# The first half of the first norm: the row's gain on VectorE, its root in a diagonal on TensorE, with other banks and another order for the convolutions

## The chip, the cores and the metric

The kernel runs on one core of one Trainium2 chip. The metric is the device time of one execution in microseconds (us), and lower is better. A core has five engines that run their own instruction streams and wait for each other by semaphores: TensorE (PE in the profile, with its weight loads as PEld), VectorE (DVE), ScalarE (ACT), GpSimd (POOL) and SyncE (SP), which here issues the loads of the weights.

## The reference

A block of a language model and a second block behind it, for 256 tokens of 1024 features, all in fp32. What lies at the change is the start of the first block:

```python
h = rmsnorm(x, norm_mix[l])            # x * rsqrt(mean(x*x) + EPS) * gain, by row
(fq, fk, fv, ff, gq, gk, gv, gb, ga, gz, sq, sk, sv, gates) = split_projection(h @ w_in[l])
...
qkv = jax.nn.silu(causal_dwconv(jnp.concatenate([gq, gk, gv], axis=-1), gdn_conv[l]))   # 4 taps
cq, ck, cv = jnp.split(qkv, [GDN_KW, 2 * GDN_KW], axis=-1)
beta = jax.nn.sigmoid(gb.astype(f32))
g_log = -jnp.exp(gdn_a_log[l].astype(f32)) * jax.nn.softplus((ga + gdn_dt_bias[l]).astype(f32))
```

Behind it come three attentions, a cross attention and three feed-forward networks, which the change doesn't touch.

## The kernel before

**Products.** An fp32 product is made of three fast ones. Each weight is split into HI, its rounding to the fast type, and LO = RAW - HI, and so is the activation (XH, XL); XH·HI, XL·HI and XH·LO are added up in PSUM. The weights come in 187 blocks of 128 x 2048, numbered through all phases: blocks 0 to 5 are `gdn` (query, key and value of the convolution), 6 to 9 `sbqk`, 10 and 11 `sbv`. A block is loaded by SyncE in two halves into one of two RAW slots, ScalarE makes its HI and VectorE its LO in one of four ring places; `split_ahead(phase, Turn(j))` does this for the block four later. GpSimd makes LO of blocks 0, 5 and 7. SyncE issues the load of a half as soon as LO of the same half two blocks earlier is made, since that frees the RAW slot.

**Order.** There is no scheduler. Every engine's order is the order of the code in its own function, and semaphores join them. A bank of ACCP (four PSUM banks of 512 columns) takes the sums of one `gdn` or `sbqk` block; TensorE waits until the bank's last reader has finished. The small results go through the four banks of SMP in the fixed order of the list `SMALL`; each waits for the bank's user four places earlier. `gTk1` so waits for `tiny`, and `gTv0` for `gTq0`.

**The opening.** X is loaded in two tiles of 128 rows (t = 0, 1). For each, ScalarE sums the squares of the first 512 columns (b = 0) and VectorE those of the last 512 (b = 1). GpSimd adds the two and takes the power -1/2: the root of each row. TensorE meanwhile spreads the gain vector over all 128 rows by a product with a row of ones (two products, one for each 512 columns, counted by `gain_spread`), and makes some idle products, `spin`. `mix_scale(t, b)` on VectorE makes XS = X x root x gain, `mix_turn(t, b)` on TensorE transposes its four 128x128 tiles, `mix_split(t, b)` takes XH from them on ScalarE and then XL on VectorE. The order of the four parts is (0,0), (1,0), (0,1), (1,1). `first_gemm` starts when XH of both b = 0 parts and the first 512 columns of HI of block 0 (`first_hi`) are there.

**The convolution banks.** For each of the six `gdn` blocks j, ScalarE copies the sums to CONVF scaled by the last tap ("base"), two copies; VectorE adds the three other taps of both feature tiles from the bank, six linked steps at L2301, and frees the bank; ScalarE applies the silu. Between the steps stand the splits of block j + 4. The `tinyT` product behind block 4 makes the narrow columns, ScalarE copies them to TINY, TensorE turns them as `tiny`, and VectorE sums them up behind its splits. When all six silus are done, TensorE turns CONVF: `gTq0`, `gTq1`, `gTk0`, `gTk1` behind `sbqk` 0, `gTv0` and `gTv1` behind `sbqk` 1.

## Time and profile before

| | |
|---|---|
| median of 3 timed runs | 1151.31 us (1149.84, 1151.31, 3620.2) |
| profiled execution, own time | 1150.2 us |
| its span | 1148.5 us |
| TensorE busy | 1137.1 us, 99% of the span |
| VectorE, ScalarE, GpSimd busy | 741.6, 589.4, 105.7 us |
| granted clock of TensorE, mean | 0.999 |
| HBM traffic | 207.67 MB read, 182 GB/s over the span |

The span runs from the first to the last instruction of the profiled execution; 1.7 us lie around it. A busy time counts overlapping instructions once. One of the three timed runs is an outlier, so the median is the higher of the two others. The rows below give start and duration in us from the start of the span.

### The profile page before, as it was taken

How to read it: one execution, taken by the hardware profiler on the slowest of the kernel's cores; microseconds unless marked ns; L12 is line 12 of the kernel's file. 1: busy time of each engine (PE TensorE's matmuls, PEld its weight loads, DVE VectorE, ACT ScalarE, POOL GpSimd, SP SyncE). 2: the span in 40 equal slices, each digit the busy share in tenths (PEclk: the TensorE clock that was granted, in tenths of full speed). 3: DMA queues.
4: the chain of work that ended last, by engine and by line, in shares of the span. 5: the costliest groups of instructions: out<-in, count | busy, mean ns of one | idle time of the engine just before them, and what ended most of it. 6: DMA issues, size and time to landing. Idle time of an engine off the chain costs nothing.

```text
span 1148.5 us, 16462 instructions
## 1 busy us (share of the span) xinstructions
PE 1137.1 (99%) x6408; PEld 993.3 (86%) x6408; DVE 741.6 (65%) x931; ACT 589.4 (51%) x788; POOL 105.7 (9%) x162
## 2 busy tenths in 40 slices
PE   9999999999999999999999999999999999999997
PEld 8998888888889999988888898899888888889885
DVE  6866686657777888754664554665866566545465
ACT  5674654446565766543554443564554364444353
POOL 6410211000011000000000000200500010000020
PEclk9999999999999999999999999999999999999999
DMA  9643753455634765564665656465457467555641
GB/s 252 206 156 97 223 185 110 164 201 184 217 132 138 251 207 176 187 215 147 209 214 182 186 174 209 154 213 181 145 187 239 146 229 234 192 168 175 213 137 72
DMA packets 122894, 209.81 MB, mean 183 GB/s; under 512 B 10965, under 2 KB 58186, under 8 KB 122827
## 3 DMA queue, kind: packets, MB, share of 16 engines
q1 hardware_dynamic: 119225, 198.64, 54.2%
q10 hardware_dynamic: 3506, 10.23, 2.4%
q8 instruction: 47, 0.77, 0.3%
q0 software_dynamic: 96, 0.01, 0.1%
q14 instruction: 20, 0.16, 0.0%
HBM read 207.67 MB, written 1.18 MB: 182 GB/s over the span
## 4 chain that ended last, share of the span: by engine, by line
PE 94%; DVE 3%; DMA 1%; ACT 1%; issue 0%; POOL 0%; POOLq 0%; DVEq 0%; SPq 0%; ACTq 0%
PE ACCP L867 28%; PE ACCP L869 28%; PE ACCP L868 28%; PE SMP L1068 3%; DVE CONVF L2301 1%; PE SMP L1061 1%; DVE LO L2176 1%; DMA RAW<-in_w_in_dram 1%; DMA X<-in_x_dram 0%; PE SMP L1221 0%; PE SMP L1237 0%; PE SMP L1021 0%; PE SMP L1016 0%; PE SMP L1015 0%; PE SMP L1406 0%
## 5 line engine op out<-in xcount | busy, mean ns | idle before, releaser
L2176 DVE TENSOR_TENSOR LO<-RAW,HI 128x1024 fp32r<-128x1024 f32 x365 | 438.1, 1237 | 231.3 <-ACT HI L1607 225.0
L1607 ACT ACTIVATE HI<-RAW 128x1024 fp32r<-128x1024 f32 x366 | 370.1, 1054 | 269.6 <-PE ACCP L869 222.6
L867 PE MATMUL ACCP<-HI,XH 128*128 128x512 f32 x704 | 277.4, 394 | 0.0
L869 PE MATMUL ACCP<-HI,XL 128*128 128x512 f32 x704 | 274.4, 390 | 0.0
L868 PE MATMUL ACCP<-LO,XH 128*128 128x512 f32 x704 | 274.0, 389 | 0.0
L867 PE MATMUL ACCP<-XH,HI 128*128 128x256 f32 x640 | 182.0, 284 | 0.7 <-DVE CONVF L2301 0.7
L869 PE MATMUL ACCP<-XH,LO 128*128 128x256 f32 x640 | 181.1, 283 | 0.0
L868 PE MATMUL ACCP<-XL,HI 128*128 128x256 f32 x640 | 181.1, 283 | 0.0
L869 PEld LDWEIGHTS ACCP<-HI,XL 128*128 128x128 f32 x704 | 132.1, 188 | 27.8
L868 PEld LDWEIGHTS ACCP<-LO,XH 128*128 128x128 f32 x704 | 132.3, 188 | 26.2
L867 PEld LDWEIGHTS ACCP<-HI,XH 128*128 128x128 f32 x704 | 132.3, 188 | 26.2
L867 PE MATMUL ACCP<-HI,HH 128*128 128x512 f32 x328 | 128.1, 390 | 0.0
L868 PE MATMUL ACCP<-LO,HH 128*128 128x512 f32 x328 | 127.7, 389 | 0.0
L869 PE MATMUL ACCP<-HI,HL 128*128 128x512 f32 x328 | 127.6, 389 | 0.0
L867 PEld LDWEIGHTS ACCP<-XH,HI 128*128 128x128 f32 x640 | 122.8, 192 | 1.0 <-issue 0.8
L868 PEld LDWEIGHTS ACCP<-XL,HI 128*128 128x128 f32 x640 | 122.8, 192 | 0.1
L869 PEld LDWEIGHTS ACCP<-XH,LO 128*128 128x128 f32 x640 | 122.8, 192 | 0.0
L715 POOL TENSOR_SCALAR STAT<-STAT 128x1 f32<-128x1 f32 (+3 forms) x24 | 10.2, 426 | 755.1 <-ACT XS L1877 449.9
L869 PEld LDWEIGHTS ACCP<-HI,HL 128*128 128x128 f32 x328 | 61.6, 188 | 12.8
L867 PEld LDWEIGHTS ACCP<-HI,HH 128*128 128x128 f32 x328 | 61.6, 188 | 12.5
L868 PEld LDWEIGHTS ACCP<-LO,HH 128*128 128x128 f32 x328 | 61.6, 188 | 12.5
L1615 ACT ACTIVATE XH<-SMP 128x512 fp32r<-128x512 f32 x36 | 20.4, 596 | 35.4 <-PE SMP L1068 35.1
(416 smaller groups left out, 1144.5 us busy)
## 6 DMA issues: line engine op xcount, KB each, us to landing
RAW<-in_w_in_dram SPq DMA_DIRECT2D x104, 512.0 KB, 4.5
RAW<-in_w_up_dram SPq DMA_DIRECT2D x44, 512.0 KB, 4.4
RAW<-in_ffn_w_gate_dram SPq DMA_DIRECT2D x44, 512.0 KB, 4.6
RAW<-in_ffn_w_up_dram SPq DMA_DIRECT2D x44, 512.0 KB, 4.5
RAW<-in_ffn_w_down_dram SPq DMA_DIRECT2D x44, 512.0 KB, 4.4
RAW<-in_w_down_dram SPq DMA_DIRECT2D x22, 512.0 KB, 4.2
RAW<-in_w_out_dram SPq DMA_DIRECT2D x8, 512.0 KB, 4.4
RAW<-in_w_mkv_dram SPq DMA_DIRECT2D x8, 512.0 KB, 4.3
```

What stands on the lines that cost most here:

```text
L715: link(pool.tensor_scalar(mean_square, mean_square, EPS, None, ALU.add))
L867: pe.matmul(dst, lhs[0], rhs[0], start=start, stop=False)
L868: pe.matmul(dst, lhs[0], rhs[1], start=False, stop=False)
L869: return pe.matmul(dst, lhs[1], rhs[0], start=False, stop=stop)
L1061: last = pe.matmul(small(name)[:, h * P:(h + 1) * P], lhs, rhs, start=True, stop=True)
L1068: last = pe.transpose(small(name)[:, h * P:(h + 1) * P], source(h), IDENT[:, :])
L1607: act.activation(HI[:, n % RING, half_of(half)], RAW[:, n % RAWS, half, :], ACT.Copy).then_inc(hi_ready, 1)
L1615: act.activation(dst, src, ACT.Copy, scale=scale).then_inc(signal, 1)
L2176: dve.tensor_tensor(LO[:, s, c], RAW[:, n % RAWS, half, :], HI[:, s, c].bitcast(f32), ALU.subtract).then_inc(lo_ready[s], 1)
L2301: ins = dve.scalar_tensor_tensor(out=y, in0=u[:, 0:SEQ - back], scalar=col("gdn_conv", (3 - back) * 12 + tile), in1=y, op0=ALU.mult, op1=A ...
```

## The change

For b = 0 VectorE multiplies X by the gain alone (`mix_scale`), right behind the square of the same tile, with a wait for the first spreading product and for ScalarE's square (which uses XS as scratch). GpSimd multiplies the identity by the row's root behind each root, into a new tile ROOT_DIAG (a 128x128 diagonal for each t). `mix_turn(t, 0)` is no transpose by the identity but four products XS^T x ROOT_DIAG, which turn the tile and scale its rows' columns by the root in one. The b = 1 parts stay as they were. ScalarE takes XH of (1,0) ahead of the first rounding of block 0.

The `gdn` blocks use ACCP banks 2, 3, 0, 1, 2, 3 in place of 0, 1, 2, 3, 0, 1, and the spreading and the idle products swap to banks 0, 1 and 2. In the convolutions ScalarE copies the bases of block j before the silu of block j - 1, and VectorE makes LO of blocks 8 and 9 behind the taps of block 5.

```diff
--- before.py
+++ after.py
@@ -124,7 +124,7 @@
                 acc(phase, j, 0, j)
         else:
             for j in range(count):
-                acc(phase, j, j, (j + (phase == "up") * 2) % 4)
+                acc(phase, j, j, (j + (phase in ("gdn", "up")) * 2) % 4)
 
 
 _accumulations()
@@ -298,6 +298,7 @@
         BIG_NOT_BEFORE = at("BIG_NOT_BEFORE", 29, [P, SEQ + P])
         TINY = at("TINY", 26, [P, SEQ])
         GAIN_ROW, ONE_ROW = at("GAIN_ROW", 64, [P, DM]), at("ONE_ROW", 68, [P, P])
+        ROOT_DIAG = at("ROOT_DIAG", 69, [P, NT, P])
         TW = at("TW", 80, [P, KT, 12])
         THL = at("THL", 81, [P, KT, 32], f32r)
         THI, TLO = THL[:, :, 0:12], THL[:, :, 12:24]
@@ -388,7 +389,7 @@
         half_sumsq = sem("half_sumsq")
         first_sq, last_product = sems("first_sq last_product")
         gain_zeroed, gain_row_loaded, gain_spread = sems("gain_zeroed gain_row_loaded gain_spread")
-        mix_sq, one_zeroed, one_row_ready, first_hi, first_lo = sems("mix_sq one_zeroed one_row_ready first_hi first_lo")
+        mix_sq, one_zeroed, root_diag, one_row_ready, first_hi, first_lo = sems("mix_sq one_zeroed root_diag one_row_ready first_hi first_lo")
         tiny_hi, tiny_lo, tiny_abs, tiny_ln, tiny_sp, tiny_exp = sems("tiny_hi tiny_lo tiny_abs tiny_ln tiny_sp tiny_exp")
         conv_base, conv_done = sems("conv_base conv_done")
         heads_sq, heads_sums, heads_ready, root_ready = sems("heads_sq heads_sums heads_ready root_ready")
@@ -729,6 +730,8 @@
                     pool.wait_ge(sumsq, t + 1)
                     link(pool.tensor_tensor(total, total, MIX_SS[:, t:t + 1], ALU.add))
                     pool.tensor_tensor(ROOT[f"{r}.{t}"], total, MINUS_HALF[:, 0:1], ALU.pow).then_inc(root_ready, 1)
+                    pool.wait_ge(root_ready, t + 1)
+                    pool.tensor_tensor(ROOT_DIAG[:, t, :], IDENT[:, :], ROOT[f"{r}.{t}"].broadcast_to([P, P]), ALU.mult).then_inc(root_diag, 1)
                     return
                 if r == "norm_ffn":
                     first = FFN_SS[:, t:t + 1]
@@ -914,7 +917,7 @@
 
             def spin(times):
                 for _ in range(times):
-                    pe.matmul(ACCP[:, 0, 0:P], ONE_ROW[:, :], ONE_ROW[:, :], start=True, stop=True)
+                    pe.matmul(ACCP[:, 2, 0:P], ONE_ROW[:, :], ONE_ROW[:, :], start=True, stop=True)
 
             def f_gemm(phase, t, xh, xl, ready=None):
 
@@ -1089,14 +1092,21 @@
             def mix_turn(t, b):
 
                 pe.wait_ge(scaled, MIX_TURNS.index((t, b)) + 1)
-                turn_four(f"norm_mix.{t}{b}", lambda k: XS[:, t, (4 * b + k) * P:(4 * b + k + 1) * P])
+                if b:
+                    turn_four(f"norm_mix.{t}1", lambda k: XS[:, t, (4 + k) * P:(5 + k) * P])
+                    return
+                pe.wait_ge(root_diag, t + 1)
+                for k in range(4):
+                    last = pe.matmul(small(f"norm_mix.{t}0")[:, k * P:(k + 1) * P], XS[:, t, k * P:(k + 1) * P], ROOT_DIAG[:, t, :],
+                                     start=k == 0, stop=k == 3)
+                finish(last)
 
             pe.wait_ge(one_row_ready, 1)
             spin(SPIN_LOAD)
             pe.wait_ge(gain_zeroed, 1)
             pe.wait_ge(gain_row_loaded, 16)
             for b in range(2):
-                pe.matmul(ACCP[:, 2 + b, :], ONE_ROW[0:97, :], GAIN_ROW[0:97, b * 512:(b + 1) * 512], start=True, stop=True).then_inc(gain_spread, 1)
+                pe.matmul(ACCP[:, b, :], ONE_ROW[0:97, :], GAIN_ROW[0:97, b * 512:(b + 1) * 512], start=True, stop=True).then_inc(gain_spread, 1)
             spin(SPIN_SPREAD)
             pe.wait_ge(masks_ready, 1)
             mix_turn(0, 0)
@@ -1670,9 +1680,9 @@
                 act.activation(XS[:, t, 0:512], X[:, t, 0:512], ACT.Square, scale=DM ** -0.5,
                                accum_out=SS["norm_mix"][:, t:t + 1]).then_inc(sumsq, 1)
             mix_split(0, 0)
+            mix_split(1, 0)
             act.wait_ge(raw_ready[0][0], 16)
             act.activation(HI[:, 0, 0:512], RAW[:, 0, 0, 0:512], ACT.Copy).then_inc(first_hi, 1)
-            mix_split(1, 0)
             act.activation(HI[:, 0, 512:1024], RAW[:, 0, 0, 512:1024], ACT.Copy).then_inc(hi_ready, 1)
             mix_split(0, 1)
             split(0, (1,))
@@ -1690,14 +1700,14 @@
             for j in range(6):
                 if j == 5:
                     take_small("tinyT", TINY[0:24, :], small("tinyT")[0:24, 0:SEQ])
-                if j:
-                    conv_silu(j - 1)
                 acc_is_done(act, "gdn", Turn(j))
                 for i in range(2):
                     for cols in range(3):
                         small_is_taken(act, f"cols{cols}")
                     copy(CONVF[:, 2 * j + i, :], acc("gdn", Turn(j))[:, i * 256:(i + 1) * 256], conv_base,
                          col("gdn_conv", 3 * 12 + 2 * j + i))
+                if j:
+                    conv_silu(j - 1)
                 split_ahead("gdn", Turn(j))
             conv_silu(5)
 
@@ -2249,9 +2259,14 @@
             def mix_scale(t, b):
 
                 part = slice(512 * b, 512 * b + 512)
+                if b == 0:
+                    dve.wait_ge(gain_spread, 1)
+                    dve.wait_ge(sumsq, t + 1)
+                    dve.tensor_tensor(XS[:, t, part], X[:, t, part], ACCP[:, 0, :], ALU.mult).then_inc(scaled, 1)
+                    return
                 root = root_is_ready(f"norm_mix.{t}")
                 dve.wait_ge(gain_spread, b + 1)
-                dve.scalar_tensor_tensor(out=XS[:, t, part], in0=X[:, t, part], scalar=root, in1=ACCP[:, 2 + b, :],
+                dve.scalar_tensor_tensor(out=XS[:, t, part], in0=X[:, t, part], scalar=root, in1=ACCP[:, b, :],
                                          op0=ALU.mult, op1=ALU.mult).then_inc(scaled, 1)
 
             def mix_split(t, b):
@@ -2266,8 +2281,7 @@
                 dve.wait_ge(x_loaded[t], 16)
                 dve.tensor_tensor_reduce(out=XS[:, t, 512:DM], in0=X[:, t, 512:DM], in1=X[:, t, 512:DM], scale=1.0 / DM, scalar=EPS,
                                          op0=ALU.mult, op1=ALU.add, accum_out=MIX_SS[:, t:t + 1]).then_inc(mix_sq, 1)
-            mix_scale(0, 0)
-            mix_scale(1, 0)
+                mix_scale(t, 0)
             mix_scale(0, 1)
             mix_split(0, 0)
             mix_split(1, 0)
@@ -2303,7 +2317,10 @@
                         if i == 0 or back < 3:
                             link(ins)
                 ins.then_inc(acc_bank("gdn", Turn(j)), 1)
-                split_ahead("gdn", Turn(j))
+                if j < 4:
+                    split_ahead("gdn", Turn(j))
+            split_ahead("gdn", Turn(4))
+            split_ahead("gdn", Turn(5))
 
             small_is_done(dve, "tiny")
             dve.wait_ge(masks_ready, 2)

```

VectorE in the opening, before, from the first square on (ISA at L2267 is the square with its sum, at L2254 stands `mix_scale`, at L2261 `mix_split`):

```order
L2267 ISA XS,STAT<-X 128x512 [waits x_loaded0]
L2267 ISA STAT 128x1
L2267 ISA XS,STAT<-X 128x512 [waits x_loaded1]
L2267 ISA STAT 128x1
L2254 SCALAR_TENSOR_TENSOR XS<-X,STAT,ACCP 128x512 [waits gain_spread,root_ready] x3
L2261 TENSOR_TENSOR XL<-SMP,XH 128x4x128 [waits norm_hi] x2
```

and now (L2282 is the square, L2265 the scaling by the gain alone, L2269 that with the root, L2276 `mix_split`):

```order
L2282 ISA XS,STAT<-X 128x512 [waits x_loaded0]
L2282 ISA STAT 128x1
L2265 TENSOR_TENSOR XS<-X,ACCP 128x512 [waits sumsq,gain_spread]
L2282 ISA XS,STAT<-X 128x512 [waits x_loaded1]
L2282 ISA STAT 128x1
L2265 TENSOR_TENSOR XS<-X,ACCP 128x512 [waits sumsq,gain_spread]
L2269 SCALAR_TENSOR_TENSOR XS<-X,STAT,ACCP 128x512 [waits gain_spread,root_ready]
L2276 TENSOR_TENSOR XL<-SMP,XH 128x4x128 [waits norm_hi] x2
```

The scaling (0,0) moved ahead of the second square, and (1,0) directly behind it.

ScalarE in the opening, before, from the second square on (L1615 takes XH, L1674 and L1676 round the first two quarters of block 0):

```order
L1670 ACTIVATE XS,STAT<-X 128x512 [waits x_loaded1]
L1615 ACTIVATE XH<-SMP 128x4x128 [waits small_done]
L1674 ACTIVATE HI<-RAW 128x512 [waits raw_ready00]
L1615 ACTIVATE XH<-SMP 128x4x128 [waits small_done]
L1676 ACTIVATE HI<-RAW 128x512
L1615 ACTIVATE XH<-SMP 128x4x128 [waits small_done]
```

and now (L1625 takes XH, L1685 and L1686 round):

```order
L1680 ACTIVATE XS,STAT<-X 128x512 [waits x_loaded1]
L1625 ACTIVATE XH<-SMP 128x4x128 [waits small_done] x2
L1685 ACTIVATE HI<-RAW 128x512 [waits raw_ready00]
L1686 ACTIVATE HI<-RAW 128x512
L1625 ACTIVATE XH<-SMP 128x4x128 [waits small_done]
L1607 ACTIVATE HI<-RAW 128x1024 [waits raw_ready01]
```

The first rounding moved from between the two XH copies of the b = 0 parts to behind both.

VectorE at the end of the convolutions, before (L2301 is a tap of block 5, L2176 a LO half, first of block 8, then of block 9, L2312 and L2313 the sums of `tiny`, after which its bank is free):

```order
L2176 TENSOR_TENSOR LO<-RAW,HI 128x1024 [waits hi_ready] x2
L2301 SCALAR_TENSOR_TENSOR CONVF<-ACCP,COL,CONVF 128x255 [waits conv_base]
L2301 SCALAR_TENSOR_TENSOR CONVF<-ACCP,COL,CONVF 128x254 [waits dve_step]
L2301 SCALAR_TENSOR_TENSOR CONVF<-ACCP,COL,CONVF 128x253 [waits dve_step]
L2301 SCALAR_TENSOR_TENSOR CONVF<-ACCP,COL,CONVF 128x255 [waits dve_step]
L2301 SCALAR_TENSOR_TENSOR CONVF<-ACCP,COL,CONVF 128x254 [waits dve_step]
L2301 SCALAR_TENSOR_TENSOR CONVF<-ACCP,COL,CONVF 128x253 [waits dve_step]
L2176 TENSOR_TENSOR LO<-RAW,HI 128x1024 [waits hi_ready] x2
L2312 TENSOR_TENSOR STAT<-SMP,STAT 128x24 [waits tiny_loaded,masks_ready,small_done]
L2313 TENSOR_TENSOR STAT<-STAT,SMP 128x24 [waits dve_step]
```

and now (L2315 a tap of block 5, L2186 LO halves, L2329 and L2330 the sums of `tiny`):

```order
L2315 SCALAR_TENSOR_TENSOR CONVF<-ACCP,COL,CONVF 128x255 [waits conv_base]
L2315 SCALAR_TENSOR_TENSOR CONVF<-ACCP,COL,CONVF 128x254 [waits dve_step]
L2315 SCALAR_TENSOR_TENSOR CONVF<-ACCP,COL,CONVF 128x253 [waits dve_step]
L2315 SCALAR_TENSOR_TENSOR CONVF<-ACCP,COL,CONVF 128x255 [waits dve_step]
L2315 SCALAR_TENSOR_TENSOR CONVF<-ACCP,COL,CONVF 128x254 [waits dve_step]
L2315 SCALAR_TENSOR_TENSOR CONVF<-ACCP,COL,CONVF 128x253 [waits dve_step]
L2186 TENSOR_TENSOR LO<-RAW,HI 128x1024 [waits hi_ready] x4
L2329 TENSOR_TENSOR STAT<-SMP,STAT 128x24 [waits tiny_loaded,masks_ready,small_done]
L2330 TENSOR_TENSOR STAT<-STAT,SMP 128x24 [waits dve_step]
```

The two LO halves of block 8 moved from ahead of the six taps to behind them.

## Rows read from the trace of the kernel before

**Rows 1.** The page: busy time by engine, and the granted clock in 40 slices.

```profile
PE 1137.1 (99%) x6408; PEld 993.3 (86%) x6408; DVE 741.6 (65%) x931; ACT 589.4 (51%) x788; POOL 105.7 (9%) x162
...
PEclk9999999999999999999999999999999999999999
```

**Rows 2.** TensorE's waits, whole span: total us, times, longest; five rows, first and last.

```profile
PE ACCP L917 <- POOL ONE_ROW L706: 1.3, 1, 1.3
...
PE SMP L1130 <- ACT TINY L1615: 0.3, 1, 0.3
```

**Rows 3.** Timeline of TensorE in the opening: start us, us, instruction, records.

```profile
3.61 1.75 PE L1099 MATMUL ACCP<-GAIN_ROW,ONE_ROW 97*128 97x512 f32 x2
...
6.05 0.61 PE L917 MATMUL ACCP<-ONE_ROW 128*128 128x128 f32 x4
...
8.24 0.66 PE L1068 MATMUL SMP<-IDENT,XS 128*128 128x128 f32 x4 [0.17 <-DVE XS L2254]
...
9.59 1.28 PE L910 MATMUL ACCP<-XH,HI 128*128 128x256 f32 x8
```

**Rows 4.** Timeline of VectorE: the squares of tiles 0 and 1.

```profile
4.45 0.69 DVE L2267 CUSTOM_DVE_ANT_0 XS<-X 128x512 f32<-128x512 f32 x1 [2.45 <-DMA X<-in_x_dram]
...
5.72 0.69 DVE L2267 CUSTOM_DVE_ANT_0 XS<-X 128x512 f32<-128x512 f32 x1 [0.57 <-DMA X<-in_x_dram]
```

**Rows 5.** Timeline of ScalarE in the opening.

```profile
7.89 0.60 ACT L1615 ACTIVATE XH<-SMP 128x512 fp32r<-128x512 f32 x1 [1.45 <-PE SMP L1068]
8.39 0.62 ACT L1674 ACTIVATE HI<-RAW 128x512 fp32r<-128x512 f32 x1
8.94 0.60 ACT L1615 ACTIVATE XH<-SMP 128x512 fp32r<-128x512 f32 x1
```

**Rows 6.** Timeline of GpSimd: sums and roots (L731), then LO of block 0.

```profile
5.35 0.19 POOL L730 TENSOR_TENSOR STAT<-STAT 128x1 f32<-128x1 f32 x1 [3.18 <-ACT XS L1670]
5.62 0.55 POOL L731 TENSOR_TENSOR STAT<-STAT 128x1 f32<-128x1 f32 x1
...
6.85 0.55 POOL L731 TENSOR_TENSOR STAT<-STAT 128x1 f32<-128x1 f32 x1
9.09 5.07 POOL L782 TENSOR_TENSOR LO<-RAW,HI 128x512 fp32r<-128x512 f32 x4 [1.68 <-ACT HI L1674]
```

**Rows 7.** Timelines: rounding of block 2's second half, and its first product on TensorE.

```profile
19.95 1.06 ACT L1597 ACTIVATE HI<-RAW 128x1024 fp32r<-128x1024 f32 x1 [2.85 <-DMA RAW<-in_w_in_dram]
...
22.33 0.39 PE L867 MATMUL ACCP<-XH,HI 128*128 128x256 f32 x1
```

**Rows 8.** Timeline of TensorE at the end of the convolutions.

```profile
47.22 0.28 PE L869 MATMUL ACCP<-XH,LO 128*128 128x256 f32 x1
...
48.78 0.36 PE L867 MATMUL ACCP<-XH,HI 128*128 128x256 f32 x1 [0.69 <-DVE CONVF L2301]
...
56.51 0.66 PE L1068 MATMUL SMP<-IDENT,CONVF 128*128 128x128 f32 x4 [0.38 <-DVE STAT L2313]
...
62.76 1.03 PE L1068 MATMUL SMP<-IDENT,CONVF 128*128 128x128 f32 x8
```

**Rows 9.** Timeline of VectorE there: LO of block 8, taps of block 5, LO of 9.

```profile
48.55 2.35 DVE L2176 TENSOR_TENSOR LO<-RAW,HI 128x1024 fp32r<-128x1024 f32 x2
50.82 3.06 DVE L2301 SCALAR_TENSOR_TENSOR CONVF<-ACCP,COL,CONVF 128x255 f32<-128x255 f32 x6
53.80 2.35 DVE L2176 TENSOR_TENSOR LO<-RAW,HI 128x1024 fp32r<-128x1024 f32 x2
```

**Rows 10.** The chain that ended last: a weight half from its issue to its use.

```profile
30.31 4.37 DMA RAW<-in_w_in_dram
```

**Rows 11.** Timeline of ScalarE: bases of block 5, HI of block 10, gTq0.

```profile
49.21 0.82 ACT L1615 ACTIVATE CONVF<-ACCP,COL 128x256 f32<-128x256 f32 x2
...
55.30 2.00 ACT L1607 ACTIVATE HI<-RAW 128x1024 fp32r<-128x1024 f32 x2
...
61.19 1.07 ACT L1615 ACTIVATE GT<-SMP 128x512 f32<-128x512 f32 x2
```

## The prediction

> **What bounds the kernel now.** I read the page's busy times first. TensorE is busy for 99% of the span [rows 1], and the line of the granted clock is full in every slice. Only two things can therefore move the end: TensorE work added or removed, and TensorE waits. The list of TensorE's waits over the whole span comes second. It has only five entries, from 1.3 us down to 0.3 us [rows 2], and all of them lie before 57 us. After that the engine runs without a gap to the end, so a shift of TensorE at about 63 us should arrive at the end unchanged. The third view is the timeline of the first 63 us, engine by engine. It has two stretches that matter here. One is the opening up to the first projection matmul at 9.59 us [rows 3]. The other is the end of the convolution banks, where TensorE waits 0.3 us for TINY [rows 2], 0.69 us for the taps of block gdn 4, whose bank it wants again, and 0.38 us for the bank of `tiny` [rows 8].
>
> **Part 1, the opening.** The change lets VectorE scale the first halves with the gain alone, without waiting for the root. Before, the scaling of (0,0) could not start until the second square was done at about 6.4 us. Now it needs only the first gain product, which is complete 1.75 us after 3.61, at 5.36 us [rows 3]. Scaling (0,0) then takes about 0.7 us, to 6.1. It stands ahead of the second square, which would start at 6.1 and not at 5.72 [rows 4]. The second square so ends at 6.8 and not at 6.41: 0.4 us later. That square feeds the second root.
>
> The root is still needed, on another path. GpSimd makes root 0 at 5.62 + 0.55 = 6.17 us [rows 6], and then a new 128x128 product, the diagonal. No such product is in the trace. The bounds are its neighbours, the same operation on fewer and on more columns: 0.19 us for the 128x1 sum that precedes the root, and 5.07/4 = 1.27 us for a 128x512 difference [rows 6]. The straight line between them gives 0.19 + 1.08 x 128/512 = 0.46 us. I take 0.45. Diagonal 0 is ready at 6.65. Root 1 ends 0.4 us later than before, 7.40 + 0.4 = 7.8, and diagonal 1 is ready at about 8.3.
>
> On TensorE the turn of (0,0) can start at 6.7 us, half a microsecond sooner than before, but a turn is now four plain fp32 products instead of four transposes. The trace shows what that means: a transposing group of four leaves four records in 0.66 us, whereas two plain fp32 128x128 products leave four records in 0.61 us [rows 3]. So four plain ones leave eight records, 1.1 us. Turn (0,0) ends at 7.85, as before, and ScalarE takes it at 7.9, as before. Turn (1,0) waits for diagonal 1 and runs from 8.35 to 9.45; before it ran from 8.24 to 8.90 [rows 3]. The gain of the early scaling is thus eaten, and turn (1,0) is 0.55 us late.
>
> Behind this stands the moved ScalarE instruction. Before, ScalarE filled its wait for turn (1,0) with the first rounding of weights, 8.39 to 9.01 us, and took (1,0) at 8.94 [rows 5]. Now that rounding stands behind (1,0): copy 9.5 to 10.0, rounding 10.0 to 10.6. TensorE's first projection matmul needs both, and starts at 10.65, not 9.59: **1.05 us late**. With the bounds on the diagonal it would be 0.75 to 2.5 late.
>
> **What the late rounding reaches.** GpSimd's four remainders of block 0 begin at 10.65 and not at 9.09 [rows 6], 1.55 us late. TensorE runs about 1.0 us late through blocks 0 and 1, always behind them. But the RAW halves of block 2 are only loaded once these remainders are made. The second of them arrived for ScalarE at 19.95 us, its remainder was made from 21.05, and TensorE started block 2 at 22.33 [rows 7], with no time to spare. If that landing moves by the full 1.55, block 2 starts at about 23.8; if it was held up by other transfers and does not move, TensorE itself is free at 23.1 to 23.3. So the shift behind the opening is +0.8 to +1.5 us, and I take +1.1. Blocks 3 to 5 had their remainders well before their turn and bring nothing.
>
> **Part 2, the convolution banks.** The banks move on by two, so the sbqk blocks take banks that were freed long before. ScalarE copies the base of block j before it runs the silu of j-1, so VectorE no longer waits for a base ahead of the taps of blocks 2 and 4. This removes TensorE's 0.69 us. The 0.3 us for TINY goes as well, because TensorE arrives 1.1 us later while ScalarE does not. TensorE issues the last product of block gdn 5 at 47.22 and is done with it 0.12 later, at 47.34 [rows 8]; now this is 48.45 us. It then turns `tiny` and starts sbqk 0 at 48.8, level with before (48.78). Up to here the two parts cancel.
>
> The price is in the moved remainders. Before, VectorE made LO of block 8 (2.35 us) ahead of the taps of block 5, at a time when it would have waited for TensorE anyway, and LO of block 9 behind them [rows 9]. Now both stand behind the taps of block 5, and these cannot start before gdn 5 is done and its two bases are copied, which takes 0.82 us [rows 11]: 48.5 + 0.85 = 49.35. The taps take 3.1, to 52.45; four remainders follow, a pair of which held the engine for 50.82 - 48.55 = 2.27 us, to 57.0; and two short sums free the bank of `tiny` 0.36 later (before, from 53.80 + 2.35 to 56.51), at 57.35. TensorE's fourth turn behind sbqk 0 waits for that; before, it started at 56.51 [rows 8]. It is now 0.85 us late, and the wait is about 1.3 us, not 0.38.
>
> Further behind: RAW of block 10 goes into the slot that block 8 frees. Its second half could be issued once LO 8 was made, 50.9 us before, 54.75 now. A weight half takes 4.37 us from issue to use in this stretch [rows 10], so it lands at 59.15. Before, ScalarE rounded block 10 at 55.30 to 57.3 without waiting; now it ends at 60.2. In ScalarE's fixed order the masks, two table loads and then the copy of gTq0 follow: that copy began 61.19 - 57.3 = 3.9 us behind the rounding [rows 11], now at 64.1, ending at 64.65. The turn of gTv0 uses its bank, and TensorE started it at 62.76 [rows 8]. So it starts at 64.7, **1.95 us late**, 1.1 of it in a new wait. Beyond this point the chains through ScalarE and VectorE (rates, heads) are about 2.4 us late where TensorE is 1.95 late, and they had some 2 us in hand, so I count nothing more.
>
> **Sum.** The profiled execution took 1150.2 us (span 1148.5, and 1.7 around it); 1150.2 + 1.95 = 1152.2 us. The three timed runs are 1149.84, 1151.31 and an outlier, so their median stands 1.1 above the profiled execution, and that much is the noise. The change is 0.2%, far inside the 2% that a measurement of this kernel can tell from no change. **Forecast: 1152.2 us, no measurable change, on the slow side.**
>
> **A rule that speaks against the diagonal.** The square of tile 1 on VectorE reads two SBUF operands. In the trace it took 0.69 us although GpSimd's root 0 ran from 5.62 to 6.17 across its start, and the undisturbed square of tile 0 took 0.69 too [rows 4, 6]: no blocking shows for one-column operations. The Trainium skill (SBUF — State Buffer, section "SBUF: two separate sides") says that a VectorE operation with two SBUF inputs and a GpSimd operation that reads SBUF exclude each other for the whole instruction. By that rule diagonal 0 would wait for the moved square to end. A wide GpSimd product in that place is something that the trace of before does not show.
>
> **Rivals.**
> 1. *The square and the diagonal exclude each other.* Diagonal 0 starts at 6.8, ends at 7.25, root 1 starts only then and ends at 8.05, diagonal 1 at 8.5: 0.2 us more on TensorE's path, up to 0.5 if the square also waits for root 0. Time 1152.4 to 1152.7. The equal 0.69 us speak against it. Chance 0.15.
> 2. *Faster: the opening costs nothing and the banks pay.* If a diagonal costs 0.19 us and the transfers hide the rest of the opening, the waits of 0.69 and 0.38 us go: 1150.2 - 1.1 = 1149.1. It also needs RAW 10 not to be late. Against it: the taps of block 5 cannot start before gdn 5 ends, which is arithmetic of the order, not of a duration. Chance 0.12.
> 3. *Clearly slower: the clock falls in the opening.* The granted clock was full behind the spins, and before, a gap of 0.69 us did not lower it [rows 1, 8]. Now TensorE idles about 0.6 us ahead of the first gemm. Should it be granted 1.2 GHz there, the six groups of eight products of block 0 (the first took 1.28 us with its tail [rows 3]; some 6 us together) would take up to twice as long: 1152.2 + 3 to 6 = 1155 to 1158. It decides at an idle time longer than those of the trace; slower by 2% (23 us) would need 46 us at the low level, nearly the whole way from the opening to the end of the banks. Chance 0.06, and 0.01 for over 2%.
> 4. *The change does not do what it says*: turn (0,0) starts no sooner than 7.23 because its diagonal is late (1.0 us or more a product). Then everything in the opening is 1.5 to 2.5 late: 1153.0 to 1153.8. Chance 0.07.
>
> The forecast itself, with its own bounds (0.8 to 1.5 from the opening, plus 0.5 to 1.2 from the banks), has the remaining 0.60.
>
> **Range.** The bounds of the forecast give 1151.5 to 1152.9; with the noise of 1.1 us of single medians and the near ends of rivals 2 and 4 it becomes 1149.6 to 1154.2. Left out are rival 3 and part of rival 2. Faster by over 2% 0.01, within 2% 0.98, slower by over 2% 0.01.
>
> **What would show it.** In the profile of the changed kernel: scaling (0,0) at 5.4 us on VectorE; a GpSimd product of 0.4 us behind each root; eight records a turn; the first projection matmul at 10.65; block 2 at 23.1 to 23.8; no wait of TensorE for CONVF; a wait for STAT of about 1.3 us near 57 us; a wait of ScalarE for w_in near 58 us; a wait of TensorE of about 1 us ahead of the gTv turns. The prediction is wrong if the first projection matmul is not later than before, or if the wait for STAT has shrunk. Then the time should be at or below 1150.

## The result, and the profile after

The changed kernel takes **1155.4 us**, the median of six executions (1153.99 to 1156.24); the kernel before takes 1150.42. The ratio is 1.0042 [1.0032, 1.0052]: a change of less than 2%, but a slowdown of 3.7 to 6.0 us by its interval, which excludes 1. The forecast was 1152.2 in a range from 1149.6 to 1154.2. The direction was right, and the time is above the range. The profiled execution of after took 1153.99 us (span 1152.2), 3.7 us of span more than before.

The page still shows an engine at 99% and a full clock in every slice, as [rows 1] did:

```profile
PE 1138.7 (99%) x6416; PEld 994.6 (86%) x6416; DVE 742.6 (64%) x931; ACT 589.8 (51%) x788; POOL 107.5 (9%) x164
PEclk9999999999999999999999999999999999999999
```

TensorE's waits over the whole span (total us, times, longest), to be held against [rows 2]:

```profile
PE SMP L1071 <- ACT GT L1625: 1.8, 1, 1.8
PE SMP L1071 <- DVE STAT L2330: 1.4, 1, 1.4
PE ACCP L920 <- POOL ONE_ROW L707: 1.3, 1, 1.3
PE ACCP L913 <- ACT HI L1685: 0.6, 1, 0.6
PE ACCP L870 <- DVE LO L2186: 0.3, 1, 0.3
```

The waits for CONVF and TINY are gone, as forecast. The wait for gTq0's bank (GT) is new, the one for the tiny sums (STAT) has grown from 0.4 to 1.4 us, and two small ones in the opening and at block 1 are new (0.6 for HI, 0.3 for LO). All lie ahead of 67 us.

TensorE, from the opening to the first matmul of block 1 (start us, us, instruction, records):

```profile
3.62 3.62 PE L1109 MATMUL ACCP<-GAIN_ROW,ONE_ROW 97*128 97x512 f32 x4
7.03 0.85 PE L920 MATMUL ACCP<-ONE_ROW 128*128 128x128 f32 x4
7.71 1.06 PE L1100 MATMUL SMP<-ROOT_DIAG,XS 128*128 128x128 f32 x8
8.83 1.06 PE L1100 MATMUL SMP<-ROOT_DIAG,XS 128*128 128x128 f32 x8
11.19 1.19 PE L913 MATMUL ACCP<-XH,HI 128*128 128x256 f32 x8 [0.64 <-ACT HI L1685]
18.44 0.39 PE L870 MATMUL ACCP<-XH,HI 128*128 128x256 f32 x1 [0.34 <-DVE LO L2186]
```

The turns have the eight records that were forecast. The first projection matmul comes at 11.19, not 9.59 [rows 3], and that of block 1 at 18.44; in the trace of before it starts at 16.42. ScalarE beside it, against [rows 5]:

```profile
8.81 0.60 ACT L1625 ACTIVATE XH<-SMP 128x512 fp32r<-128x512 f32 x1 [2.29 <-PE SMP L1100]
9.93 0.60 ACT L1625 ACTIVATE XH<-SMP 128x512 fp32r<-128x512 f32 x1 [0.52 <-PE SMP L1100]
10.42 0.62 ACT L1685 ACTIVATE HI<-RAW 128x512 fp32r<-128x512 f32 x1
```

GpSimd there, against [rows 6]:

```profile
6.28 0.84 POOL L734 TENSOR_TENSOR ROOT_DIAG<-IDENT,STAT 128x128 f32<-128x128 f32 x1
7.98 0.40 POOL L734 TENSOR_TENSOR ROOT_DIAG<-IDENT,STAT 128x128 f32<-128x128 f32 x1
11.12 5.05 POOL L785 TENSOR_TENSOR LO<-RAW,HI 128x512 fp32r<-128x512 f32 x4 [2.74 <-ACT HI L1685]
```

The two diagonals are the same instruction and took 0.84 and 0.40 us. VectorE's rows, against [rows 4, 9], show what lay beside the first: its second square. Below it stand the low halves of block 1, beside GpSimd's 5.05 us, and then the taps and the low halves at the end of the banks:

```profile
5.57 0.69 DVE L2265 TENSOR_TENSOR XS<-X,ACCP 128x512 f32<-128x512 f32 x1 [0.39 <-PE ACCP L1109]
6.17 0.68 DVE L2282 CUSTOM_DVE_ANT_0 XS<-X 128x512 f32<-128x512 f32 x1
...
15.38 3.00 DVE L2186 TENSOR_TENSOR LO<-RAW,HI 128x1024 fp32r<-128x1024 f32 x2 [0.25 <-ACT HI L1607]
...
50.27 3.07 DVE L2315 SCALAR_TENSOR_TENSOR CONVF<-ACCP,COL,CONVF 128x255 f32<-128x255 f32 x6 [1.80 <-ACT CONVF L1625]
53.26 4.62 DVE L2186 TENSOR_TENSOR LO<-RAW,HI 128x1024 fp32r<-128x1024 f32 x4
```

The chain that ended last passes through exactly this place (start us, us, what), against [rows 10], where the transfer took 4.37:

```profile
53.26 2.36 DVE LO L2186 x2
55.62 0.02 issue
55.64 5.24 DMA RAW<-in_w_in_dram
60.87 0.02 issue
60.89 1.06 ACT HI L1617
```

ScalarE waits for the two halves of that load and comes late to gTq0, against [rows 11]:

```profile
58.59 1.06 ACT L1617 ACTIVATE HI<-RAW 128x1024 fp32r<-128x1024 f32 x1 [2.41 <-DMA RAW<-in_w_in_dram]
60.89 1.06 ACT L1617 ACTIVATE HI<-RAW 128x1024 fp32r<-128x1024 f32 x1 [1.25 <-DMA RAW<-in_w_in_dram]
...
65.85 0.58 ACT L1625 ACTIVATE GT<-SMP 128x512 f32<-128x512 f32 x1
```

TensorE comes late to the fourth turn and to the turn of v (the eight transposes of `gTv0` and `gTv1`), against [rows 8]:

```profile
58.24 0.66 PE L1071 MATMUL SMP<-IDENT,CONVF 128*128 128x128 f32 x4 [1.39 <-DVE STAT L2330]
...
66.48 1.09 PE L1071 MATMUL SMP<-IDENT,CONVF 128*128 128x128 f32 x8 [1.83 <-ACT GT L1625]
```

The turn of v starts at 66.48, not 62.76: 3.72 us late, and the span is 3.7 longer. The span minus the start of v's turn is a ruler for all that follows: it is 1148.5 - 62.76 = 1085.7 before and 1152.2 - 66.48 = 1085.7 after.

### The profile page after: what moved, and what is told of

The parts are those of the page before. It is cut to its first block, busy times and chain, and to the rows that moved or that the text cites. A ratio compares the mean times of both kernels' runs of the same rounds, so it can differ in the third digit from the quotient of the medians.

```text
span 1152.2 us, 16485 instructions
## 1 busy us (share of the span) xinstructions
PE 1138.7 (99%) x6416; PEld 994.6 (86%) x6416; DVE 742.6 (64%) x931; ACT 589.8 (51%) x788; POOL 107.5 (9%) x164
## 4 chain that ended last, share of the span: by engine, by line
PE 96%; DVE 1%; ACT 1%; DMA 0%; issue 0%; POOL 0%; POOLq 0%; DVEq 0%; ACTq 0%
PE ACCP L870 29%; PE ACCP L872 29%; PE ACCP L871 29%; PE SMP L1071 3%; PE SMP L1064 1%; DVE LO L2186 1%; DMA RAW<-in_w_in_dram 0%; PE SMP L1247 0%; PE SMP L1231 0%; PE SMP L1024 0%; PE SMP L1019 0%; PE SMP L1018 0%; PE SMP L1416 0%; PE SMP L1512 0%; PE SMP L1395 0%; PE ACCP L1109 0%
## 5 line engine op out<-in xcount | busy, mean ns | idle before, releaser
L2186 DVE TENSOR_TENSOR LO<-RAW,HI 128x1024 fp32r<-128x1024 f32 x365 | 439.0, 1240 | 233.0 <-ACT HI L1617 227.4
L1625 ACT ACTIVATE XH<-SMP 128x512 fp32r<-128x512 f32 x36 | 20.4, 596 | 36.7 <-PE SMP L1071 33.6
```

Source lines behind the costliest of these rows:

```text
L1625: act.activation(dst, src, ACT.Copy, scale=scale).then_inc(signal, 1)
L2186: dve.tensor_tensor(LO[:, s, c], RAW[:, n % RAWS, half, :], HI[:, s, c].bitcast(f32), ALU.subtract).then_inc(lo_ready[s], 1)
```

## The experiments

Fourteen kernels, their medians beside the kernel before run on the same chip (1150.21 to 1150.32 in these groups). "v" is the start of v's turn in the profiled execution, "rest" the span minus it.

| kernel | median us (executions) | ratio | v | rest |
|---|---|---|---|---|
| lo_back | 1150.22 (11) | 1.0000 [0.9991, 1.0009] | 62.44 | 1085.7 |
| hi_back | 1154.94 (5) | 1.0045 [1.0031, 1.0059] | 65.36 | 1085.7 |
| lo_hi_back | 1149.38 (11) | 0.9991 [0.9982, 1.0000] | 61.73 | 1085.8 |
| conv_only | 1152.65 (9) | 1.0023 [1.0013, 1.0033] | 64.41 | 1085.8 |
| opening_only | 1151.80 (11) | 1.0014 [1.0005, 1.0023] | 63.94 | 1085.7 |
| diag_only | 1151.03 (11) | 1.0006 [0.9997, 1.0015] | 62.96 | 1085.7 |
| lo_only | 1155.59 (5) | 1.0044 [1.0030, 1.0057] | 66.33 | 1087.5 |
| banks_silu | 1148.39 (11) | 0.9984 [0.9975, 0.9993] | 60.85 | 1085.7 |
| tiny_first | 1155.87 (5) | 1.0052 [1.0038, 1.0066] | 66.76 | 1087.2 |
| gt_early | 1152.82 (11) | 1.0024 [1.0015, 1.0033] | 64.25 | 1086.7 |
| diag_waits | 1156.22 (1) | | 66.93 | 1087.4 |
| spin_gap | 1154.46 (5) | 1.0036 [1.0022, 1.0049] | 66.32 | 1085.7 |
| lo_spin | 1154.62 (5) | 1.0036 [1.0022, 1.0049] | 66.69 | 1085.8 |
| tiny_spin | 1155.45 (5) | 1.0042 [1.0028, 1.0056] | 67.23 | 1086.5 |

### Halves and single undos

**lo_back** undoes one move of the change:

```
-                if j < 4:
-                    split_ahead("gdn", Turn(j))
-            split_ahead("gdn", Turn(4))
-            split_ahead("gdn", Turn(5))
+                split_ahead("gdn", Turn(j))
```

> The changed kernel with one edit undone: VectorE makes LO of block 8 ahead of the taps of block gdn 5 again, and LO of block 9 behind them. Theory (the chain behind the moved LO halves): both new waits go (1.4 us for STAT near 58 us, 1.8 us for gTq0's bank near 66 us), RAW of block 10 lands near 55.5 us, the gTv turns start at about 62.8 us as in the kernel before, and the time is 3 to 4 us below the changed kernel's, 1150 to 1151.5 us. Rival (the loss is made in the opening, by the late first matmul and the clock that rises later): the time stays above 1153 us.

Measured 1150.22, level with the kernel before. The waits for STAT and GT are both gone, and v's turn stands at 62.44. The move of two instructions carries the whole loss, and the rest of the change comes out at nothing. As the runs below show, that nothing is a gain of 1.9 us and two losses that add up to as much.

**hi_back** puts ScalarE's first rounding back between the two copies of XH.

```
             mix_split(0, 0)
-            mix_split(1, 0)
             act.wait_ge(raw_ready[0][0], 16)
             act.activation(HI[:, 0, 0:512], ...)
+            mix_split(1, 0)
```

> The changed kernel with one edit undone: ScalarE rounds the first 512 columns of block 0 between the two XH copies again. Theory: GpSimd's LO of block 0 begins some 1 to 1.5 us earlier than in the changed kernel, the first projection matmul 0.5 us earlier, block gdn 2 starts 0.5 to 1 us earlier, and since everything behind hangs on it, the time is 0.5 to 1.2 us below the changed kernel's, about 1154.5 us. Rival (all of the opening's loss comes from this move): the time falls by 2 us or more.

Measured 1154.94, with 1152.97 to 1157.01 among five executions, so the median settles little. Its trace, whose own time is 1152.97 (1153.99 in that of after), does: the first projection matmul comes at 10.33 with no wait, block 1 at 17.12 (18.44 in after), v's turn 1.12 us sooner at 65.36, and the wait for GT has grown to 2.0 us.

**conv_only** and **opening_only** are the two parts of the change, each alone on the kernel before. conv_only is the three edits `(j + (phase in ("gdn", "up")) * 2) % 4`, `conv_silu(j - 1)` behind the base copies, the swap of banks for the spreading and the idle products that goes with the first, and the low halves as above; opening_only is the scaling by the gain, the diagonals and ScalarE's order.

> The kernel before with the second part of the change alone: gdn banks moved on by two, base copies ahead of the silu, LO of blocks 8 and 9 behind the taps of block 5; the opening as before. Theory: no wait for CONVF, a wait for STAT of about 1.2 us, a wait for gTq0's bank of 1 to 1.9 us; gTv turns at 64 to 64.7 us; time 1 to 2 us above before, 1151.5 to 1152.5. Rival (the banks' part pays for itself, the loss is the opening's): time at or below before's.

> The kernel before with the first part alone: gain on VectorE, root diagonal, first rounding behind both XH copies; convolutions and banks as before. Theory: first projection matmul at 10.7 to 11.2 us, block gdn 2 at 23.5 to 24.2, everything behind it late by that 1.2 to 1.9 us; time 1151.7 to 1152.5. Rival (the opening's loss is taken up by the waits that follow it): no difference from before, under 0.5 us.

Measured 1152.65 and 1151.80, +2.35 and +1.5 us against 1150.3, together 3.85 of the change's 5; conv_only lies 0.15 above what was expected. Neither part was free, and the second part, which I had put at +0.85 (1.95 less 1.1), is the larger.

**banks_silu** is conv_only without the move of the low halves.

> The kernel before with two edits of the change alone: the gdn banks moved on by two, and the base copies ahead of the silu of the block before. Opening and VectorE's LO order as before. Theory: these two are the gain in the change, the same 1.5 us that made up for the opening in lo_back: no wait for CONVF, none or under 0.2 us for STAT, none for gTq0's bank, sbqk 0 at 47.7 us, gTv turns at 61 us instead of 62.8; time 1148.6 to 1149.2 us. Rival (TensorE arriving earlier only waits elsewhere, for STAT or gTq0's bank): within 0.5 us of before.

Measured 1148.39, 1.9 us under the kernel before, the fastest of all, and clear of 1 by its interval. TensorE's rows in its trace have no wait behind them:

```profile
53.35 1.91 PE L1068 MATMUL SMP<-IDENT,CONVF 128*128 128x128 f32 x16
60.85 0.82 PE L1068 MATMUL SMP<-IDENT,CONVF 128*128 128x128 f32 x6
```

All sixteen records of the q and k turns follow one another, where [rows 8] had a wait of 0.38 before the last four. This is rival 2's gain of the banks, and larger than the 1.1 us that I gave it: v's turn is 1.91 us sooner, of which the three waits that are gone (0.69, 0.38 and 0.32 for TINY) are 1.39. No run separates the banks from the order of base copy and SiLU, so which of the two brings the gain is not shown. The move of the low halves on top costs 1152.65 - 1148.39 = 4.3 us.

**lo_hi_back** undoes both moves, **diag_only** leaves scaling and diagonals alone on the kernel before, and **lo_only** moves nothing but the low halves there.

> The changed kernel with two moves undone: VectorE takes the low half of block 8 ahead of the taps of block 5 again, and ScalarE rounds the first quarter of block 0 between the two copies of XH again. Theory: with the low half back the two waits for the scan's banks are gone (1150.2 us was measured for that alone), and the rounding's old place starts the first projection 0.4 to 0.9 us sooner, all of which reaches the end: 1149.3-1149.8 us. Rival: the opening's gain is given back to a wait at the convolution's end, or the rounding's late place costs nothing: 1150.0-1150.4 us.

> The kernel before with the row-only scaling and the two diagonals on GpSimd alone; banks, order of the SiLU, of the low half and of ScalarE's first rounding as before. Theory: the diagonals alone delay the opening by 0.6 to 1.2 us (they run beside VectorE's squares at 0.6 to 0.9 us in place of 0.4), and what is delayed there reaches the end: 1151.0-1151.5 us, under the 1151.8 us of the whole opening part since the rounding keeps its place. Rival: the opening's cost comes from the rounding's new place alone, and the diagonals are hidden: 1150.2-1150.6 us.

> The kernel before with one move: the low halves of blocks 8 and 9 behind the taps of block 5. Theory: the end of that chain (taps, low halves, the buffer for block 10, its load, its rounding, the copy of gTq0) sets the turns of v, and stands some 0.7 us later than in the kernel with banks and SiLU changed too, since the products of block 5 still wait for their bank: v's turns at 65.0-65.6 us, 1153.2-1153.8 us, 1.4 us more where the clock falls behind the wait. Rival: the move costs by itself only the wait for the first of the scan's banks (1.4 us), since the old waits hide the rest: 1151.5-1152.0 us.

Measured 1149.38 and 1151.03, both as the theory had them. The diagonals cost 1149.38 - 1148.39 = 1.0 us on the new banks and 0.8 on the old, where the interval includes no change. No run separates the scaling by the gain from the diagonals. ScalarE's moved rounding costs 1150.22 - 1149.38 = 0.84, and 1151.80 - 1151.03 = 0.8 on the old banks. lo_only was dearer than theory and rival: 1155.59, of which 1.7 are the clock (below). Step by step from before to after it is 1150.3 - 1.9 (banks and SiLU) + 1.0 (diagonals) + 0.84 (rounding) + 5.2 (low halves, 1155.4 - 1150.22) = 1155.4. Such a sum of differences must add up; that the sizes are right is seen from v's turn in the five traces, which moves by -1.91, +0.88, +0.71 and +4.04.

### The waits at the end of the banks

**tiny_first** puts the two tiny sums between the low halves of block 8 and those of block 9, and so ends the wait for STAT alone.

```
             split_ahead("gdn", Turn(4))
-            split_ahead("gdn", Turn(5))
...
             dve.tensor_tensor(TY, TY, tiny[:, :, 12:24], ALU.add)...
+            split_ahead("gdn", Turn(5))
```

> The changed kernel, but VectorE makes the two sums that free the bank of tiny between LO of block 8 and LO of block 9. The wait for STAT (1.4 us) so goes; LO of block 8, and the load of block 10 behind it, stay as late. Theory (the last of the two waits alone counts, which comes over the load of block 10): the wait for gTq0's bank grows from 1.8 to about 3.2 us, and the time stays within 0.5 us of the changed kernel's 1155.4. Rival (both waits add up): 1.4 us less, 1154.0.

The wait for STAT is gone, the one for GT has become 4.0 us (3.2 were expected; the transfer took 5.75 us where it took 5.24 in after), and v's turn starts at 66.76. What TensorE no longer waited for STAT it waited for GT: what counts is when gTq0 is copied. The median is 1155.87, no better.

**gt_early** copies gTq0 on ScalarE ahead of the rounding of block 10, so that the late transfer is no longer between TensorE and v's turn.

```
+            take_small("gTq0", GT[:, 0, 0, :], small("gTq0"))
             split_ahead("sbqk", Turn(0))
...
-            take_small("gTq0", GT[:, 0, 0, :], small("gTq0"))
```

> The changed kernel, but ScalarE copies gTq0 out of its bank right behind the copy of sbqk 0, ahead of the rounding of block 10 that waits for the late load. Theory: the wait for gTq0's bank goes (1.8 us in the changed kernel's profile), that for STAT stays at 1.4; the time falls by about 1.8 us to 1153.6, if the rates, which ScalarE makes behind the same rounding, are still in time. Rival (the late rounding reaches TensorE over the rates or heads in any case): a wait of 1 us or more appears at the gcol or gFk products, and the time falls by less than 0.8.

The new wait is gone and v's turn starts at 64.25, 2.2 us sooner; 1.4 of wait for STAT remain. The median falls by 2.6 to 1152.82. Some 1.0 us is given back behind it (rest 1086.7). Held against after, TensorE's matmuls are 2.23 us sooner at v's turn, 1.7 at 75.5 us, behind a wait of 0.3 us for ScalarE's copy of GT, and 1.26 at 312 us; what takes the last 0.4 is open.

**diag_waits** lets GpSimd wait for both squares before the first diagonal; it has one execution only.

```
                     pool.wait_ge(root_ready, t + 1)
+                    pool.wait_ge(mix_sq, 2)
```

> The changed kernel, but GpSimd waits for both squares of VectorE before it makes a diagonal. Theory (VectorE's square with two SBUF inputs and the GpSimd product exclude each other; without it the product takes 0.40 us): diagonal 0 starts at about 6.9 us instead of 6.3, takes 0.40 us instead of 0.84, and is ready within 0.2 us of when it was. Rival (diagonal 0 is long for a reason of its own, such as the first use of the operation): it still takes over 0.7 us.

GpSimd's first diagonal now lies behind the square, and takes what the second always took:

```profile
7.00 0.40 POOL L735 TENSOR_TENSOR ROOT_DIAG<-IDENT,STAT 128x128 f32<-128x128 f32 x1 [0.78 <-DVE STAT L2283]
```

So the other 0.44 us in after were spent on VectorE's square. Two more readings say the same. In the nine traces in which the first diagonal began inside the square, it took 0.57 to 0.88 us, less the later in the square it began, and always ended 0.25 to 0.27 us behind the square. And in tiny_spin, where the second tile of X came late and the square began at 6.53, the first diagonal ran from 6.30 in 0.40 us with the same code of the opening: the first use of the instruction is not what makes it long. The wait doesn't gain here: the result comes at 7.40 instead of 7.12.

### The clock behind the wait

The spans of tiny_first, lo_only and diag_waits are 1.5 to 1.8 us longer than the ruler allows. The windows of lo_only show why (columns: stretch, its length, busy time of PE, PEld, DVE, ACT, POOL, then the granted clock, DMA share, GB/s):

```profile
66.00:68.00 2.00, 1.67 (x13) 1.68 (x14) 0.01 (x1) 2.00 (x4) 0.00 (x0) 0.87 0.05 15
68.00:70.00 2.00, 2.00 (x11) 2.00 (x11) 1.77 (x2) 1.98 (x3) 0.00 (x0) 0.50 0.00 0
```

The same stretch in after:

```profile
66.00:68.00 2.00, 1.52 (x13) 1.52 (x14) 0.16 (x1) 2.00 (x4) 0.00 (x0) 1.00 0.11 41
68.00:70.00 2.00, 2.00 (x19) 2.00 (x18) 1.62 (x2) 1.98 (x3) 0.00 (x0) 1.00 0.00 0
```

Eleven matmuls fit where nineteen did: 1.2 GHz, not 2.4, from 67.5 to 70.9 us in lo_only, behind a wait of 1.93 us. It cost 1087.5 - 1085.7 = 1.8 us. The same trace had waited 1.95 us for STAT before, and there the clock stayed full:

```profile
56.00:58.00 2.00, 0.05 (x2) 0.01 (x1) 1.93 (x5) 0.00 (x0) 0.00 (x0) 1.00 0.92 308
```
 The mean clock of each execution is a hint whether it happened there too. In after it is 0.996, 0.996 and 0.997 in three executions (1156.24, 1155.41, 1155.45 us) and 0.998 or 0.999 in the other three (1153.99, 1154.26, 1155.39). A fall of 3.4 us takes 1.7 of 1152, 0.0015, from the mean, which fits. The profiled one is of the second kind. That the first kind holds such a fall is read from the means alone and not shown, since after was profiled once; four of the 76 executions of the kernel before have 0.996 or 0.997 too, without this wait.

Three kernels fill the wait with products whose result is overwritten (eight, in tiny_spin sixteen; ones by ones, into the bank that the third scan projection takes next); nothing of the computation is left out:

```
             f_gemm("sbqk", Turn(1), XH, XL)
+            acc_banks_free(pe, "sbqk", Turn(2))
+            spin(8)
             for t in range(NT):
                 turn_four(f"gTv{t}", ...)
```

> The changed kernel with eight idle products (128x128 of ones, into the accumulator bank that the third scan projection overwrites) between the second scan projection and the first turn of v, so that TensorE works where it waits for gTq0's bank to be copied. Eight such products take some 1.7 us at the full clock, under the wait of 1.8 us. Nothing else is changed. Theory: the wait itself costs what it did, and behind it the granted clock falls to its lower level in most executions (for 3.4 us, as in the two traces with waits of 2.2 and 4.0 us), which costs them 1.2 to 1.7 us; with the engine kept busy the clock stays full, the start of the turn of v stays at 66.5 us, and the median falls from 1155.4 to 1153.9-1154.6 us. Rival: the executions over 1154 us lose their time elsewhere (the opening's clock rises late, a DMA lands late); then the median stays at 1155.2-1155.6 us.

> The kernel before with the low halves behind the taps of block 5 (the run lo_only, 1155.59 us, whose trace shows the granted clock at the lower level from 67.5 to 70.9 us), and eight idle products of 0.2 us each between the second scan projection and the first turn of v, where TensorE waited 1.9 us for gTq0's bank. Theory: the wait itself brings the clock down; with it filled, the clock stays full, the turn of v starts where it did, and the time falls by 1.5 to 1.7 us, to 1153.9-1154.1 us. Rival: the fall has another cause at that place (the transposes themselves, or the load on the chip), stays where it is, and the time stays at 1155.4-1155.8 us.

> The changed kernel with the tiny sums between the low halves of blocks 8 and 9 (the run tiny_first, 1155.87 us, wait of 4.0 us ahead of the turn of v, the granted clock at the lower level from 67.9 to 71.3 us), and sixteen idle products, some 3.4 us at the full clock, in that wait. Theory: the clock stays full and the time falls by 1.5 to 1.7 us, to 1154.2-1154.4 us. Rival: the clock falls as before, and the time stays at 1155.6-1156.1 us.

The windows of lo_spin:

```profile
66.00:68.00 2.00, 1.80 (x17) 1.61 (x16) 0.18 (x1) 2.00 (x5) 0.00 (x0) 1.00 0.22 83
68.00:70.00 2.00, 2.00 (x19) 2.00 (x18) 1.41 (x2) 1.98 (x3) 0.00 (x0) 1.00 0.00 0
```

The fall is gone from all three traces, and the rest is back at 1085.7 and 1085.8 in spin_gap and lo_spin. Of the five executions of lo_only all had 0.996 or 0.997; of lo_spin's one had 0.997, and of spin_gap's and tiny_spin's none. So the idle time in this place is what the fall needs. The times recover less than the 1.5 to 1.7 us expected: 1.0 in lo_spin, 0.4 in tiny_spin, and 0.9 in spin_gap, which is inside what was expected there. In all three the intervals of the ratios overlap with those of the kernels without the idle products, so the traces show the effect and the times alone do not. In the profiled lo_spin v's turn was itself 0.36 us later than in lo_only, since the second tile of X came later: the square began at 6.24 against 5.85, the first projection matmul at 10.11 against 9.72. In tiny_spin the same tile came late, and v's turn is 0.47 us later than in tiny_first. Its rest of 1086.5 has 0.8 us over the ruler: against after its matmuls are 0.75 us late from v's turn to 302 us and 1.46 us at 312, at a full clock; the cause is open.

## Why the prediction was wrong

Most rows that it named to look for are there: scaling (0,0) at 5.57, eight records a turn, no wait for CONVF, the wait of 1.4 us for STAT, ScalarE's wait for w_in at 58.6, a new wait ahead of v's turn. Three came out otherwise: the first diagonal took 0.84 us and not 0.4, the first projection matmul came at 11.19 and not 10.65, and block 2 started at 24.29, outside 23.1 to 23.8. The sum was 3.2 us short of the median. The mechanism was right and two of its terms were too small; together they are the 1.77 us by which v's turn was missed (66.48, not 64.7). A third, the clock, stood at nothing.

1. **"I take +1.1" for the shift behind the opening.** It was +2.02 us at block 1, and 1.96 at block 2 (24.29 against 22.33 [rows 7]). There was no wait at block 2: the landing on which the choice between 0.8 and 1.5 was to hang moved by only 0.57 us (ScalarE's rounding at 20.52, not 19.95), and TensorE itself was late. The base copies of block 5 so ran at 49.40 in place of 48.5, and the second low half of block 8 was made at 55.64 in place of 54.75: 0.9 us. Two things are in it, and a third stands beside it.
   - The first projection matmul was called at 10.65 and came at 10.74 to 11.27 in the eight traces with the whole opening part, in after at 11.19: 0.54 us of the 0.9. In after the four records of the gain products took 3.62 us, 0.9 each; in lo_back they took 2.52, as the three behind the first took 1.66 us and not 2.77, and the matmul came at 10.74. I read that as a clock that rose later in after; the granted clock printed for this stretch is 1.00 in both, so the lengths alone say it. The sum had taken one trace's lengths [rows 3] for granted.
   - VectorE and GpSimd slowed each other where I hadn't looked. GpSimd's four remainders of block 0 began at 11.12 and ran to 16.17, beside VectorE's low halves of block 1, which took 3.00 us instead of 2.49. TensorE waited 0.34 us for them, which is the rest. I had moved these remainders by 1.55 us and asked only what they did to the load of block 2.
   - Beside it: the exclusion that rival 1 described is real. "The equal 0.69 us speak against it" was the wrong row: there a one-column root lay beside the square, and the diagonal reads 128 columns of SBUF. In after it cost TensorE nothing, since the first turn came at 7.71, behind TensorE's own products, and the diagonal was ready at 7.12. Where the gain products were short it did: TensorE stood 0.82 us behind the first diagonal in diag_only and 0.48 in lo_back.
2. **"A weight half takes 4.37 us from issue to use in this stretch".** It took 5.24 in after, and 4.79 to 5.75 in eight other traces with the low halves moved: 0.87 us more, on the path. And the row is not of this stretch: it starts at 30.31 us, some 25 us earlier. The same chain in the trace of before has another row, which took far longer:

```profile
16.39 7.23 DMA RAW<-in_w_in_dram
```

   One row was no bound. Why the transfer is longer at its new time is not shown; other transfers beside it are a guess.
3. **The clock.** Rival 3 had a fall of the clock "in the opening", behind an idle time of 0.6 us, at 0.06. The falls that the traces show, in lo_only, tiny_first and diag_waits, came behind v's wait, which the forecast itself contained at 1.1 us and priced at its own length. It grew to 1.83 us in the trace through points 1 and 2, and by their mean clocks, though by no trace, three of the six executions fell to 1.2 GHz behind it: 1.2 us between the medians of the two kinds (1155.45 and 1154.26). Rival 3's condition, an idle time longer than those of the trace, was met by my own new wait, and I didn't apply it there.

With the first two it is 1152.2 + 0.9 + 0.87 = 1154.0, which is the profiled 1153.99. The median is 1.4 us above that. The clock is the likely larger part, as spin_gap, whose trace and means hold no fall, has a median of 1154.46; but one execution of after with a mean clock of 0.999 took 1155.39, so it is not all, and the rest is open.

The accounting "Up to here the two parts cancel" was also off: sbqk 0 began at 49.52, not 48.8, again by point 1. Right were the mechanisms of part 2, in their order and with their durations (taps 3.07 of 3.1 us, four low halves 4.62 of 4.54), the 3.9 us from the rounding to gTq0 (61.95 to 65.85), and "nothing more" beyond v's turn, by the ruler of 1085.7 us. The gain from banks and SiLU (1.9 us) and the loss from the low halves (5.2) stood in one net term of +0.85 (1.95 less the 1.1 of the opening), and I didn't see that the change holds a version of itself that is faster. Rival 4 is out: the first turn came at 7.71, but behind the spins, with its diagonal ready at 7.12.

On the diagonal the Trainium skill (SBUF — State Buffer, section "SBUF: two separate sides") has it that whichever engine starts first keeps the shared ports for its whole instruction. The 0.84 us beside the square and the 0.40 us of the same instruction without it agree. Two numbers fit it less well: the diagonal ended 0.26 us behind the square and not its own 0.40, and in tiny_spin, where the diagonal began first, the square took 0.71 us, only 0.02 more than alone.

## What to carry to other kernels

When an instruction moves on a queue, follow the buffer that it frees: two subtractions moved behind the taps cost 5 us, since the load behind them, its rounding and a copy in ScalarE's fixed order all came late. Split a change that mixes gains and losses before summing it; here banks and SiLU alone are 7 us faster than the whole. And a new wait of TensorE can cost more than its length, where the clock falls behind it: keep the engine at work in it, or price both cases.

## What was unexpected of the hardware

- The granted clock fell to 1.2 GHz for 3.4 us behind waits of 1.93, 2.24 and 3.96 us ahead of v's turn (lo_only, diag_waits, tiny_first); behind waits of 1.39, 1.83 and 2.01 us in the same place of conv_only, after and hi_back it did not, nor behind waits of 1.95 and 1.96 us for STAT in lo_only and lo_spin. So the length of the wait alone does not decide it, and executions of one kernel can differ: the mean clocks of after are of both kinds. Cost: 1.5 to 1.8 us each.
- A 128x128 product on GpSimd takes 0.40 us alone and 0.84 beside a square on VectorE; a VectorE pair of 128x1024 differences takes 3.00 us beside GpSimd's differences and 2.35 without (the pair of block 1 took 2.49 in before, where GpSimd ended at 14.16, 0.3 us into it). At 38.97 us in after such a pair took 2.99 us beside two GpSimd differences that ran until 39.73, where before it took 2.35 at 38.81.
- The same opening, with the same code, put the first projection matmul at 9.58, 9.59, 9.72, 9.95 and 10.11 us in five traces (banks_silu, before, lo_only, conv_only, lo_spin). It follows the landing of X's second tile, behind which VectorE's second square began at 5.72, 5.72, 5.85, 5.96 and 6.24 us.
